# Shifting the split-operand views of a two-block transformer kernel inside their buffers

## The reference, cut to what matters

```python
# first block, once
h = rms_norm(x, norm1_w);  proj = h @ w_in            # 1024 -> 8192
...                                                   # retention, o ; gated linear recurrence, hl
y_a = (norm(o) * silu(g_ret)) @ w_ret_o               # 1024 -> 1024
r, i = sigmoid(blockwise xc @ w_r), sigmoid(xc @ w_i)
y_b = (hl * gelu(y_lru)) @ w_lru_o                    # 1024 -> 1024
x = x + mix @ w_out
gate, val = split(rms_norm(x, norm2_w) @ ffn_w_up)    # 1024 -> 6144
x = x + (gelu(conv(gate)) * val) @ ffn_w_down         # 3072 -> 1024
x = rms_norm(x, norm_f_w)
# second block, two layers
for l in range(2):
    x = x + 0.5 * rmsnorm((silu(h @ w_gate) * (h @ w_up)) @ w_down)   # 1024 -> 2 x 2816 -> 1024
    p = h @ w_in                                      # 1024 -> 2064, hybrid mixer
    x = x + rmsnorm(concat(...) @ w_out)
    x = x + 0.5 * rmsnorm((silu(h @ w_gate) * (h @ w_up)) @ w_down)
```

## Time and profile before

| | |
|---|---|
| runs before, median (lowest to highest) | 1453.62 us (1452.39 to 1457.54) |
| the profiled execution's own time | 1452.81 us |
| its span, first to last instruction | 1450.9 us |
| TensorE matmuls busy | 1423.1 us, 98% of the span |
| TensorE weight loads busy | 1247.8 us, 86% |
| VectorE busy | 968.7 us, 67% |
| ScalarE busy | 735.9 us, 51% |
| GpSimd busy | 94.5 us, 7% |

### The profile page before, as it was taken

One profiled execution on the slowest core, in us unless ns is written; L12 is line 12 of the kernel. 1 busy time (PEld: TensorE's weight loads), 2 busy tenths in 40 slices (PEclk: granted clock), 3 DMA queues, 4 the chain that ended last, 5 costly groups with the idle time before them and its releaser, 6 DMA issues. The chain is left out here.

```text
span 1450.9 us, 21310 instructions
## 1 busy us (share of the span) xinstructions
PE 1423.1 (98%) x8888; PEld 1247.8 (86%) x8888; DVE 968.7 (67%) x1165; ACT 735.9 (51%) x936; POOL 94.5 (7%) x107
## 2 busy tenths in 40 slices
PE   7999999999999999999999999999999999999998
PEld 7899999899988788888987888878888898788886
DVE  5968786688864665546977665556665579665644
ACT  5534854555643544446656444454444567544442
POOL 0001000000000000001720000000000045000000
PEclk9999999999999999999999999999999999999999
DMA  7745455667655666456334755547754462466542
GB/s 244 232 139 182 158 191 198 176 191 201 198 192 163 211 210 224 153 193 159 133 114 143 221 174 189 189 146 246 231 186 171 140 174 103 138 198 197 178 161 101
DMA packets 251411, 259.13 MB, mean 179 GB/s; under 512 B 26659, under 2 KB 213428, under 8 KB 251316
## 3 DMA queue, kind: packets, MB, share of 16 engines
q1 hardware_dynamic: 250432, 255.49, 55.5%
q10 hardware_dynamic: 884, 2.28, 0.4%
HBM read 256.69 MB, written 1.05 MB: 178 GB/s over the span
## 5 line engine op out<-in xcount | busy, mean ns | idle before, releaser
L1028 DVE TENSOR_TENSOR w_lo<-raw,w_hi 128x2048 fp32r<-128x2048 f32 x240 | 548.2, 2287 | 317.5 <-ACT w_hi L632 317.1
L632 ACT ACTIVATE w_hi<-raw 128x2048 fp32r<-128x2048 f32 x240 | 456.3, 1902 | 332.0 <-PE psm L1713 150.8
L1713 PE MATMUL stream<-a_pair,w_hi 128*128 128x256 f32 x2144 | 378.2, 280 | 3.5 <-DVE a_pair L1047 1.9
L1713 PE MATMUL stream<-w_hi,a_pair 128*128 128x512 f32 (+1 forms) x1152 | 363.4, 388 | 8.1 <-DVE w_lo L1028 5.7
L1713 PEld LDWEIGHTS stream<-a_pair,w_hi 128*128 128x128 f32 x2144 | 325.9, 188 | 6.1 <-issue 3.3
L1713 PE MATMUL stream<-a_pair,w_lo 128*128 128x256 f32 x1072 | 298.4, 278 | 0.0
L1713 PEld LDWEIGHTS stream<-w_hi,a_pair 128*128 128x128 f32 x1152 | 214.2, 188 | 53.2 <-DVE w_lo L1028 8.3
L1713 PE MATMUL stream<-w_lo,a_pair 128*128 128x512 f32 (+1 forms) x576 | 221.0, 384 | 0.0
L1713 PEld LDWEIGHTS stream<-a_pair,w_lo 128*128 128x128 f32 x1072 | 201.8, 188 | 0.0
L1713 PE MATMUL psm<-w_hi,h_hi 128*128 128x512 f32 x448 | 175.1, 391 | 0.0
L1713 PE MATMUL psm<-w_hi,h_lo 128*128 128x512 f32 x448 | 174.4, 389 | 0.0
(11 more groups left out here) (278 smaller groups left out, 1361.0 us busy)
## 6 DMA issues: line engine op xcount, KB each, us to landing
raw<-in_ffn_w_up SPq DMA_DIRECT2D x136, 512.0 KB, 5.0
raw<-in_ffn_w_down SPq DMA_DIRECT2D x104, 512.0 KB, 4.4
raw<-in_ffn_w_gate SPq DMA_DIRECT2D x88, 512.0 KB, 4.0
raw<-in_w_in SPq DMA_DIRECT2D x80, 512.0 KB, 4.7
raw<-in_w_out SPq DMA_DIRECT2D x24, 512.0 KB, 4.3
raw<-in_w_ret_o SPq DMA_DIRECT2D x8, 512.0 KB, 4.5
raw<-in_w_lru_o SPq DMA_DIRECT2D x8, 512.0 KB, 4.3
diag<-in_conv_diag SPq DMA_DIRECT2D x8, 512.0 KB, 5.8
```

The source lines that it names most:

```text
L632: nc.scalar.activation(w_hi[s][:, :, 0:n], raw[s][:, :, 0:n], ACT.Copy).then_inc(w_hi_ready, 1)
L1028: V.tensor_tensor(w_lo[s][:, :, 0:n], raw[s][:, :, 0:n], w_hi[s][:, :, 0:n].bitcast(F32), ALU.subtract).then_inc(w_split, 1)
L1713: return nc.tensor.matmul(dst, lhs, rhs, start=start, stop=stop, skip_group_check=True)
```

## The change

It gives the views other places in the same two buffers. Nothing else is edited: the same instructions in the same order, with other addresses.

```diff
-A_AT = {N_IN: 4, N_LRU: 16, N_UP1: 16, N_F: 0, N_L: 16, N_L + 1: 0, N_L + 2: 0, N_L + 3: 16, N_L + 4: 0}
-B_AT = {B_RG: 16, B_RETO: 16, B_OUT: 0, B_MIX: 0}
+A_AT = {N_IN: 48, N_LRU: 40, N_UP1: 24, N_F: 96, N_L: 18, N_L + 1: 104, N_L + 2: 116, N_L + 3: 20, N_L + 4: 80}
+B_AT = {B_RG: 28, B_RETO: 48, B_OUT: 32, B_MIX: 0}
```

## The result

The changed kernel takes 1473.22 us (median of 3 runs, 1472.30 to 1473.58) where the kernel before takes 1453.62 us: a ratio of 1.0124, with a 95% interval of 1.0101 to 1.0147. It is slower by 19.6 us. The profiled execution took 1473.22 us, with a span of 1471.4 us against 1450.9 us.

The account below looks back on a forecast made before the run. TensorE's distances between matmul starts bound the kernel. 256-column stages -1.1 us, `N_IN`'s 512-column part -0.6, gated stages 0: -1.7 on 1452.8 gives 1451.1, plus 0.8 for the median, 1452 us; range 1442 to 1465.

Parts of the forecast that it names:

- Rival C: Gated stages at new differences behave like 240, 3.5 us each; all four, with `N_UP1` slow, give 1471 us; chance 0.24.
- What bounds the kernel: Whole kernel: TensorE busy 1423.1 of 1450.9 us, so time is the sum of distances between matmul starts.
- For the gated stages I take no change, the nearest row being their own at 0: Four gated feed-forwards: priced at no change, with ends of -0.4 and +3.5 us for each.
- Each stage's cost lies between the fast pace and the slow one seen for its form: All stages: 256-column ones put at the middle of 113.4 and 117.7 ns, 7.7 us above fast against 8.8 today.
- No row shows a difference of 72, 80, 96 ...: Evidence: no row at 72, 80, 96, 112, 128 or 160 bytes, nor 48, 64 or 192 with 512 columns.
- the rest wins 3.6: 256-column stages other than `N_UP1`: win 3.6 us while `N_UP1` loses 2.5, netting -1.1 us.
- Rival A: All stages: differences near zero disturb, the new ones settle at the fast pace; 1443 to 1445 us; chance 0.25.
- Rival B: All stages: addresses play no part, stream start sets the pace; 1453.6 us plus or minus 5 us; chance 0.1.
- Rival D: All streams: new differences reach a floor below 113.4 and 226.7 ns, half of it worth 26 us, 1427 us; chance 0.03.
- The remark on the spread: The three runs' 5.1 us spread equals `N_UP1` at its other pace, and may be that very thing.
- the signs of being wrong: Wrong if `N_UP1` and `N_IN` together move by more than 5 us, or one gated stage alone by more than 4.
- The sign for C: Gated stages: a mean of 394 ns or more, and 132 us rather than 128.4 for the stage.

Follow-up runs that it names:

- experiment 2: Kernel before with only `N_UP1` moved, shift 16 to 24 (difference 96 instead of 64 bytes): 1459.62 us, ratio 1.0045.
- Experiment 1: Kernel before with only the four gated feed-forwards at their new shifts (differences 128, 96, 48, 192 bytes): 1463.65 us against 1452.73, ratio 1.0071.
- experiment 4: Kernel before with weight tiles and all views but `B_MIX` 128 bytes higher; down products' and `B_MIX` differences become 128, others stay: 1466.71 us, ratio 1.0085.
- experiment 8: Kernel before with only `N_IN` at 192 bytes (512-column part at 64) and `B_RG` at 112: 1452.31 us against 1453.23, ratio 0.9998.
- experiment 9: Kernel before with 4 and 5 more filler products in two TensorE gaps ahead of `N_UP1`: 1454.19 us, ratio 1.0004.
- experiment 10: Kernel before with `N_IN`, `N_LRU` and both mixers at 192 bytes, `B_RG` at 112, plus extra filler products ahead of `N_UP1`: 1452.08 us, ratio 0.9985.
- experiment 3: Kernel before with all the change's other shifts, gated feed-forwards and `N_UP1` left as before: 1454.06 us, ratio 1.0015.

## Why the prediction was wrong

It said 1452 us, with a range up to 1465; the time is 1473.2. Rival C, the gated stages leaving their good place, is what happened. That its full case of 1471 us came so close is in part luck: its terms were 13.9 us for the gated stages, 5.0 for `N_UP1` and -1.5 for the rest, and they measured 11.6, 7.7 and +1.5. Point by point:

- **What bounds the kernel** was right. The time is the sum of the distances between matmul starts, and the balance above puts the whole 20.5 us there. No wait took part, and the writes into the views cost nothing (the busy time of VectorE and ScalarE moved by under 1 us).
- **"For the gated stages I take no change, the nearest row being their own at 0": this step failed**, and it carries +11.6 us. The row at 0 told of 0 only. The one row of 512 columns at another difference was that at 240, and it had the price: 233.3 ns, where 128, 96, 48 and 192 now show 233.1 to 233.4. The row of the same form at another difference was the nearest one, not that of the same stage at the difference it was leaving. (That row was a lucky one: the 512-column units of `N_IN` at 240 began at 226.7 ns in experiment 2.) Experiment 1 shows the cost alone, +10.9 us. C priced a stage at 528 x 6.6 = 3.5 us; it cost 2.9, as the stages' pace before was 227.5 ns over all of their stream with its breaks, not the 226.7 of settled stretches.
- **"Each stage's cost lies between the fast pace and the slow one seen for its form"** failed too. For `N_UP1` I took half of 1152 x 4.3, 2.5 us. At a difference of 96 there is a third pace: 1152 x (120.0 - 113.33) = 7.7 us, which experiment 2 shows alone. Two paces seen at differences of 64 and 192 were no bound for differences that nobody had run. The sentence "No row shows a difference of 72, 80, 96 ..." was right, and what follows it in the prediction does not follow from it.
- **The mixers** were to win with "the rest wins 3.6"; at 72 and 80 they lost 2.3 us (121.2 and 119.5 ns), above the slow pace again.
- **`N_IN`, `B_RG`, `B_RETO` and `N_LRU`** won 1.4 us, most of it in the first units of `N_IN` (113.5 ns in every profile with a difference of 192; 113.4 to 118.7 ns at 16, so the gain depends on the execution that it is compared with) and a little in its 512-column units (229 ns at 64, not the 226.7 I took). `N_LRU` at 160 runs at 118.7 ns instead of 117.7. **`B_OUT`** lost the 0.6 us of the bound.
- **Rival A** (near zero is bad) was wrong: for 512 columns 0 itself is the best place, though 4, 8 and 252 are bad, and far from it 128 is as bad as 8; for 256 columns 0 is as bad as 96, and 64 and 192 are good. **Rival B** fell with experiments 1 and 4: equal matmuls are 5.6 ns further apart (233.1 against 227.5) by the difference of the two addresses alone. What it says of the start of a stream is right within one difference: at 64 and 192 the start picks between 113.3 and 117.8 ns. The Trainium skill, page "TensorE: Matmul & The Clock Gate", section "Part 2: What happens when you issue a matmul", has loading weights and streaming read through ports of their own; the prediction drew from it that the addresses play no part and the change is worth 0 us, and that is not what the runs show. Whether the two reads meet at a port or elsewhere, no run shows. **Rival D** found nothing for it: no stage at any of the differences tried went below 113.3 or 226.7 ns.
- **The remark on the spread** fits: 5 us are `N_UP1` at its other pace (experiment 8).
- **Of the signs of being wrong** the first came true, `N_UP1` and `N_IN` together moved by 6.0 us (+7.7 and -1.7). The second, a gated stage alone by more than 4 us, could not: the prediction's own bound for one such stage was 3.5 us. The sign for C was good: means of 395 to 398 ns in `N_F`, where 394 or more was named.
- **The chance for C**, 0.24, was too low. It "decides from about three such stages", I wrote, as if each had its own draw; but the only value seen off 0 was bad, so the four were likely to stand or fall together. The range's end took "two or three gated stages lost", and left out the case in which one rule holds for all.

## What to carry to other kernels

Where both operands of a stream of matmuls come from on-chip memory, the difference of their addresses modulo 256 bytes is a parameter that can have a price: here, with float32r operands and full 128 x 128 weights, up to 2.9% for 512 columns (233.3 against 226.7 ns) and 7.0% for 256 (121.2 against 113.3). Measure it for each matmul width before choosing: 0 was best for the one and among the worst for the other, and a place 4 or 8 bytes away said nothing of it. Look at the pace of single stretches and not only at a stage's mean, as one difference can hold two paces. And when several stages move from a measured place to unmeasured ones, price them by the rows of their form at other places, as one draw and not several.

## What the runs showed of the hardware that was not expected

- A stream of 256-column matmuls at a difference of 64 or 192 takes up one of two paces, 113.3 or 117.8 ns, when it starts, and keeps it until it is broken: but for `B_RG`, whose groups of 12 matmuls are short, no profile here has a change between the two without a break. The changed kernel's units 8 to 19 of `N_IN` (192 bytes) go from 113.3 to 117.8 ns behind one break, back behind a later one and to 117.8 again. In `N_UP1` this alone puts the runs of one and the same kernel into two groups 5 us apart (experiments 8 to 10). At 0 and 96 there is only one pace, 120.0 ns, and the runs lie within 1.5 us.
- At a difference of 0, a gated stage's stream comes back to 226.7 ns behind each break; over a whole stage the mean is 227.5 at 0, 228.0 at 16, where stretches at 226.7 alternate with stretches at about 228.3, and 232.3 at 4.
- In the profiled execution of experiment 4 the granted clock was 0.50 (1.2 GHz) for 3.4 us at the start of `N_UP1`, and 17 matmuls ran some 213 ns apart, behind a wait of 1.05 us for `a_pair`. No other profile here showed it between 272 and 284 us, though experiment 3 has the same wait of 1.05 us; it cost about 17 x (213 - 118) ns = 1.6 us. The row of the timeline behind the wait (in brackets the wait and its releaser) and the window:

```profile
274.95 0.66 PE L1714 MATMUL stream<-a_pair,w_hi 128*128 128x256 f32 x2 [1.05 <-DVE a_pair L1067]
```
```profile
275.07:278.48 3.41, 3.41 (x17) 3.41 (x18) 3.41 (x7) 2.19 (x3) 0.00 (x0) 0.50 0.00 0
```
